# RWKV entry of a two-block forward pass: three receptance weight chunks multiplied as split fp32r products, and the elementwise chain behind them in another order

## What is computed

```python
xx = _token_shift(h) - h
xr, xw, xk, xv, xa, xg = [h + xx * mu[i] for i in range(6)]
r = (xr @ w_r).astype(f32)                      # the receptance
k = (xk @ w_k).astype(f32)
v = (xv @ w_v).astype(f32)
w = -jax.nn.softplus(-(w0 + jnp.tanh(xw @ w1) @ w2).astype(f32)) - 0.5
a = jax.nn.sigmoid((a0 + (xa @ a1) @ a2).astype(f32))
...
kk = kk / jnp.maximum(jnp.sqrt(jnp.sum(kk * kk, axis=-1, keepdims=True)), 1e-12)
k = k * (1.0 + (a - 1.0) * k_a.astype(f32))
decay = jnp.exp(-jnp.exp(w))
# step: sa = state @ a_t, with a_t = -kk; state = state * decay + sa b_t + v k; y = state @ r
bonus = jnp.sum(rh * kh * r_k.astype(f32), axis=-1, keepdims=True) * vh
```

## Time and profile before

| what | value |
|---|---|
| median of 3 runs | 1225.54 us (1224.85 to 1226.44) |
| the profiled execution | 1226.66 us, of which its span from first to last instruction is 1224.9 us |
| PE busy | 1211.5 us, 99% of the span |
| DVE, ACT, POOL busy | 523.5, 607.0 and 778.9 us |
| granted TensorE clock | 1.00 of full speed (2.4 GHz) over the span |
| the stretch that the change touches | about 853 to 915 us from the span's start |

### The profile page before, as it was taken

The page is one execution under the profiler, slowest core; times in us unless marked ns, Lnnn a source line. Parts: engine busy times, 40 slices in busy tenths (PEclk is TensorE's granted clock), DMA queues, the critical chain, the costliest instruction groups (busy, mean ns, idle before and its releaser), DMA issues.

```text
span 1224.9 us, 23270 instructions
## 1 busy us (share of the span) xinstructions
PE 1211.5 (99%) x9722; PEld 1055.7 (86%) x9722; DVE 523.5 (43%) x812; ACT 607.0 (50%) x793; POOL 778.9 (64%) x200
## 2 busy tenths in 40 slices
PE   8999999999999999999999999999999999999998
PEld 7888887788898888899988888888888998888887
DVE  4232234665433233243533332239696574332233
ACT  6544443545464445486465544455421445554543
POOL 3988880154188888766468888863015535888884
PEclk9999999999999999999999999999999999999999
DMA  7655554244255555555245555553332124555551
GB/s 295 210 199 187 189 195 159 73 174 170 71 191 208 184 202 178 202 189 182 74 143 196 184 195 190 187 186 124 138 138 71 38 92 154 181 197 200 180 203 68
DMA packets 31020, 202.01 MB, mean 165 GB/s; under 512 B 3424, under 2 KB 5344, under 8 KB 7392
## 3 DMA queue, kind: packets, MB, share of 16 engines
q1 hardware_dynamic: 28064, 196.63, 45.4%
q10 hardware_dynamic: 2880, 4.26, 1.0%
HBM read 198.79 MB, written 2.10 MB: 164 GB/s over the span
## 4 chain that ended last, share of the span: by engine, by line
PE 94%; POOL 2%; DVE 1%; issue 1%; ACT 1%; DMA 1%; SPq 0%; POOLq 0%; DVEq 0%
PE psum L353 25%; PE psum L355 13%; PE psum L344 10%; PE psum L346 10%; PE psum L345 10%; PE psum L986 6%; PE psum L999 3%; PE psum L3005 2%; POOL wlo L3384 2%; PE psum L3021 1%; PE psum L341 1%; PE psum L342 1%; PE psum L343 1%; PE psum L2975 1%; PE psum L599 1%
## 5 line engine op out<-in xcount | busy, mean ns | idle before, releaser
L3384 POOL TENSOR_TENSOR wlo<-raw,whi 128x2048 fp32r<-128x2048 f32 x160 | 736.6, 4609 | 282.2 <-ACT whi L314 237.6
L353 PE MATMUL psum<-f_both,whi 128*128 128x512 f32 x1408 | 492.2, 393 | 1.7 <-DVE wlo L699 1.7
L314 ACT ACTIVATE whi<-raw 128x2048 fp32r<-128x2048 f32 x160 | 306.3, 1915 | 218.5 <-PE psum L355 169.4
L355 PE MATMUL psum<-f_both,wlo 128*128 128x256 f32 x1408 | 393.7, 280 | 0.0
L353 PEld LDWEIGHTS psum<-f_both,whi 128*128 128x128 f32 x1408 | 264.4, 188 | 60.3 <-DVE wlo L699 2.2
L355 PEld LDWEIGHTS psum<-f_both,wlo 128*128 128x128 f32 x1408 | 264.5, 188 | 1.5
L344 PE MATMUL psum<-whi,ahi 128*128 128x512 f32 x352 | 137.4, 390 | 0.3 <-POOL wlo L3384 0.3
L346 PE MATMUL psum<-whi,alo 128*128 128x512 f32 x352 | 137.0, 389 | 0.0
L345 PE MATMUL psum<-wlo,ahi 128*128 128x512 f32 x352 | 136.9, 389 | 0.0
L909 DVE TENSOR_TENSOR psum<-psum,arena 128x512 f32<-128x512 f32 x43 | 30.1, 700 | 241.8 <-ACT arena L625 241.7
L925 DVE TENSOR_TENSOR alo<-arena,ahi 128x512 fp32r<-128x512 f32 x44 | 95.2, 2163 | 31.7 <-ACT ahi L858 31.7
(11 more groups left out here) (430 smaller groups left out, 1484.6 us busy)
## 6 DMA issues: line engine op xcount, KB each, us to landing
raw<-stream SPq DMA_DIRECT2D x182, 1024.0 KB, 4.8
con<-consts SPq DMA_DIRECT2D x1, 1376.0 KB, 14.6
x<-x_in SPq DMA_DIRECT2D x1, 1024.0 KB, 5.1
raw<-stream SPq DMA_DIRECT2D x2, 512.0 KB, 7.4
kept_x<-x ACTq DMA_DIRECT2D x1, 1024.0 KB, 3.9
x<-kept_x ACTq DMA_DIRECT2D x2, 512.0 KB, 3.9
out<-x SPq DMA_DIRECT2D x4, 256.0 KB, 2.0
arena<-gm_w_s ACTq DMA_DIRECT2D x1, 512.0 KB
```

Of the source, the lines that this page charges most:

```text
L314: nc.scalar.activation(whi[:, slot, :], raw[:, c % RAW, :], ACT.Copy).then_inc(high_made, 1)
L353: nc.tensor.matmul(psum[:, bank, :].rearrange("p (a n) -> p a n", a=2), whi[w], f_both[:, :, k, :], start=k == 0, stop=False, skip_group_c ...
L355: return nc.tensor.matmul(psum[:, bank, 0:TOK], wlo[w], f_hi[:, k, :], start=False, stop=k == KT - 1, skip_group_check=True)
L3384: nc.gpsimd.tensor_tensor(part(wlo[:, slot, :]), part(raw[:, c % RAW, :]), part(whi[:, slot, :]).bitcast(F32), ALU.subtract)\
```

## The change

It has four parts; two tensors `rx_hi` and `rx_lo` are laid into unused parts of the arena for it.

1. Receptance chunks 1, 2 and 3 are split chunks. ACT makes their high parts (in the loop of the sigmoids and behind the first two receptance copies) and four high parts `rx_hi` of their input; DVE, not POOL, makes their low parts (`receptance_low`) and the low parts `rx_lo` of the input. PE multiplies them with `split_by_tiles`.
2. The exponential of the sum before the token and the subtraction for it are dropped. The decayed keys take the exponential of the running sum, read one token earlier within each chunk of 64 tokens (L2620 of the changed kernel), and the first token of each chunk is only negated (L2619). Two exponentials are left.
3. The bonus weight r_k goes into the two-column matrix (`bonus_weights`), so that `rk` is a plain product in two instructions; the bonus sums stand behind value chunk 8 and the first half of value chunk 9. The bonus copy on DVE stands behind the low parts of chunk `L2`, and the first half of the first scores waits for `rw_scaled` 1 alone.
4. On ACT all four receptance copies stand ahead of the exponentials. The value mixture (variant 5) stands right behind the norms' reciprocal on DVE.

```diff
...
-RWKV_SPLIT = [("rw", 0, j) for j in (5, 6, 7)]
+RWKV_SPLIT = [("rw", 0, j) for j in (5, 6, 7, 1, 2, 3)]
...
+        bonus_weights = s3m[:, 384:400].rearrange("p (k h) -> p k h", k=8)
...
+            for b in range(4):
+                k = slice(2 * b, 2 * b + 2)
+                eng.wait_ge(s("rw_mixed"), mixed(4, 2 * b + 1))
+                nc.scalar.activation(rx_hi[:, k, :], variant_x[0][:, k, :], ACT.Copy).then_inc(s("rw_rhi"), 1)
             eng.wait_ge(s("rw_first"), 3)
...
             for k in range(8):
+                if k == 4:
+                    highs.upto(CH[RW(1)])
                 if k % 2 == 0:
...
                 projected(eng, name)
-                eng.wait_ge(s("rw_kx"), 4)
                 read(nc.scalar.activation(rr[:, 2 * j:2 * j + 2, :], bank2(proj_bank(name)), ACT.Copy), name)
-                if j == 0:
-                    eng.wait_ge(s("rw_before"), 1)
-                    nc.scalar.activation(sw, sw, ACT.Exp, scale=-DECAY).then_inc(s("rw_exp"), 1)
-                if j == 1:
-                    eng.wait_ge(s("rw_before"), 2)
+                if j < 2:
+                    highs.upto(CH[RW(2 + j)])
+                if j == 3:
+                    eng.wait_ge(s("rw_before"), 8)
                     nc.scalar.activation(sw, sums, ACT.Exp, scale=DECAY).then_inc(s("rw_exp"), 1)
-                    eng.wait_ge(s("rw_exp"), 2)
+                    eng.wait_ge(s("rw_exp"), 1)
                     nc.scalar.activation(sums, sums, ACT.Exp, scale=-DECAY).then_inc(s("rw_exp"), 1)
...
+            r_k = vec[:, VEC_AT["r_k"]:VEC_AT["r_k"] + 8].rearrange("p (k a) -> p k a", a=1).broadcast_to((P, 8, 2))
+            heads = const("same64")[:, 0:P:64].rearrange("p (a h) -> p a h", a=1).broadcast_to((P, 8, 2))
+            steps(nc.vector.tensor_tensor(bonus_weights, r_k, heads, ALU.mult))
             steps(nc.vector.memset(ht[:, :, 0:1], 0.0))
...
             nc.vector.reciprocal(roots[:, 0:2, :], roots[:, 0:2, :]).then_inc(s("rw_unit"), 1)
+            mix_variant(5)
+
+            def receptance_low(j):
 
-            eng.wait_ge(s("rw_sig"), 16)
+                c = CH[RW(j)]
+                eng.wait_ge(high_made, LOWS[c] - 2)
+                eng.wait_ge(low_made, LOWS[c] - 1)
+                nc.vector.tensor_tensor(wlo[:, SLOT[c], :], raw[:, c % RAW, :], whi[:, SLOT[c], :].bitcast(F32), ALU.subtract)\
+                    .then_inc(low_made, 1)
+
+            for b in range(4):
+                k = slice(2 * b, 2 * b + 2)
+                eng.wait_ge(s("rw_rhi"), b + 1)
+                nc.vector.tensor_tensor(rx_lo[:, k, :], variant_x[0][:, k, :], rx_hi[:, k, :].bitcast(F32), ALU.subtract)\
+                    .then_inc(s("rw_rlo"), 1)
+            receptance_low(1)
             for k in range(8):
-                ins = nc.vector.tensor_scalar(rr[:, k, :], aa[:, k, :], 1.0, V_AT("k_a", k), ALU.subtract, ALU.mult)
+                eng.wait_ge(s("rw_sig"), 2 * k + 2)
+                ins = nc.vector.tensor_scalar(sums[:, k, :], aa[:, k, :], 1.0, V_AT("k_a", k), ALU.subtract, ALU.mult)
             steps(ins)
...
    -                nc.vector.scalar_tensor_tensor(out=kx[:, k, :], in0=rr[:, k, :], scalar=1.0, in1=kx[:, k, :],
+                nc.vector.scalar_tensor_tensor(out=kx[:, k, :], in0=sums[:, k, :], scalar=1.0, in1=kx[:, k, :],
                                                op0=ALU.add, op1=ALU.mult).then_inc(s("rw_kx"), 1)
-            for k in range(8):
-                ins = nc.vector.tensor_tensor_scan(sums[:, k, :], const("restart", TOK), sw[:, k, :], 0.0, ALU.mult, ALU.add)
-            steps(ins)
-            nc.vector.tensor_tensor(sw, sums, sw, ALU.subtract).then_inc(s("rw_before"), 1)
+
+            def up_to_token(tiles):
+                for k in tiles:
+                    nc.vector.tensor_tensor_scan(sums[:, k, :], const("restart", TOK), sw[:, k, :], 0.0, ALU.mult, ALU.add)\
+                        .then_inc(s("rw_before"), 1)
+
+            eng.wait_ge(s("rw_kx"), 4)
+            up_to_token((0,))
+            receptance_low(2)
+            up_to_token((1, 2))
+            receptance_low(3)
+            up_to_token(range(3, 8))
             eng.wait_ge(S["rw_lw"], 6)
...
             steps(nc.vector.tensor_tensor(aa, aa, kk, ALU.mult))
-            eng.wait_ge(s("rw_exp"), 1)
-            nc.vector.scalar_tensor_tensor(out=kk, in0=kk, scalar=-1.0, in1=sw, op0=ALU.mult, op1=ALU.mult).then_inc(s("rw_before"), 1)
-            mix_variant(5)
+            chunks_of = lambda v: v.rearrange("p k (c t) -> p (k c) t", c=4)
             eng.wait_ge(s("rw_exp"), 2)
+            nc.vector.tensor_scalar(chunks_of(kk)[:, :, 0:1], chunks_of(kk)[:, :, 0:1], -1.0, None, ALU.mult)
+            steps(nc.vector.scalar_tensor_tensor(out=chunks_of(kk)[:, :, 1:64], in0=chunks_of(kk)[:, :, 1:64], scalar=-1.0,
+                                                 in1=chunks_of(sums)[:, :, 0:63], op0=ALU.mult, op1=ALU.mult))
             steps(nc.vector.tensor_tensor(aa, aa, sw, ALU.mult))
...
             eng.wait_ge(s("rw_mixed"), mixed(5, 7))
-            for k in range(8):
-                nc.vector.scalar_tensor_tensor(out=rk[:, k, :], in0=rr[:, k, :], scalar=V_AT("r_k", k), in1=kx[:, k, :],
-                                               op0=ALU.mult, op1=ALU.mult).then_inc(s("rw_rk"), 1)
+            for k in (slice(0, 4), slice(4, 8)):
+                nc.vector.tensor_tensor(rk[:, k, :], rr[:, k, :], kx[:, k, :], ALU.mult).then_inc(s("rw_rk"), 4)
             eng.wait_ge(s("rw_rk"), 8)
             steps(nc.vector.tensor_tensor(kx, kx, sw, ALU.mult))
-            eng.wait_ge(s("rw_exp"), 3)
             steps(nc.vector.tensor_tensor(rr, rr, sums, ALU.mult))
...
-            eng.wait_ge(s("rw_bonus_sum"), 1)
-            nc.vector.tensor_copy(bonus, psum[:, 4, 0:32]).then_inc(s("rw_scaled"), 1)
             eng.wait_ge(high_made, LOWS[L2] - 2)
...
                 .then_inc(low_made, 1)
+            eng.wait_ge(s("rw_bonus_sum"), 1)
+            nc.vector.tensor_copy(bonus, psum[:, 4, 0:32]).then_inc(s("rw_scaled"), 1)
             centred_values(0)
...
-            def split_by_tiles(slot, bank):
+            def split_by_tiles(slot, bank, h_hi=key_hi, h_lo=key_lo, made=lambda k: eng.wait_ge(s("rw_mixed"), 8 + k // 2 + 1)):
 
                 for k in range(KT):
-                    eng.wait_ge(s("rw_mixed"), 8 + k // 2 + 1)
+                    made(k)
                     for j in range(2):
                         w = (slice(None), slot, slice(k * 256 + j * P, k * 256 + j * P + P))
-                        mm = three_passes(bank2(bank)[:, j, :], whi[w], wlo[w], key_hi[:, k, :], key_lo[:, k, :], True,
+                        mm = three_passes(bank2(bank)[:, j, :], whi[w], wlo[w], h_hi[:, k, :], h_lo[:, k, :], True,
                                           (k, j) == (0, 0), k == KT - 1, skip=True)
...
             for j in range(1, 4):
-                project(eng, RW(j), plain_columns, h=variant_x[0])
+                project(eng, RW(j), split_by_tiles, h_hi=rx_hi, h_lo=rx_lo, made=lambda k: eng.wait_ge(s("rw_rlo"), k // 2 + 1))
                 if j == 1:
...
-            def bonus_sums(half, k):
+            def bonus_sums(k):
 
-                if half == 0:
-                    return
                 eng.wait_ge(s("rw_rk"), k + 1)
...
                     mm = nc.tensor.matmul(psum[:, 4, 16 * m + 2 * k:16 * m + 2 * k + 2], rk[:, k, m * P:(m + 1) * P],
-                                          const("same64")[:, 0:P:64], start=True, stop=True)
+                                          bonus_weights[:, k, :], start=True, stop=True)
                 if k == KT - 1:
...
-            project(eng, RW(8), plain_tokens, h=value_x, wait=made(5), between=bonus_sums)
+            project(eng, RW(8), plain_tokens, h=value_x, wait=made(5))
 
...
             values_quarter(1, 1)
+            for k in range(KT):
+                bonus_sums(k)
 
...
+            eng.wait_ge(s("rw_scaled"), 1)
+            scores(0, 0, 0)
             eng.wait_ge(s("rw_scaled"), 2)
-            for q in range(2):
-                scores(0, 0, q)
+            scores(0, 0, 1)
             values_quarter(1, 2)
...
                         rwkv_pool(pool, low)
-                    elif c not in PLAIN and names[c] not in (("lora", 0, 2), ("rw_o", 0, 1)):
+                    elif c not in PLAIN and names[c] not in (("lora", 0, 2), ("rw_o", 0, 1), RW(1), RW(2), RW(3)):
                         low(c)
```

6 lines of the change are left out of this document (4 added, 2 removed).

## The result

The changed kernel takes 1228.62 us in the median of 10 runs (1227.41 to 1230.11), the kernel before beside it on the same chip 1225.5 us (10 runs, 1224.51 to 1226.51). The ratio is 1.0026, with a 95% interval of 1.0016 to 1.0035: the change makes the kernel 3.1 us slower. The forecast of 1227.1 us had the sign and half of the size. The profiled execution took 1230.11 us, 3.45 more than the one of before; its span is 1228.2 us against 1224.9. It is the longest of the ten, so the traces show how the time is made up, and the medians what the change costs.

The account below looks back on a forecast made before the run. The prediction took PE, with 94% of the chain, to bound the kernel. PE -3.6, bank's wait -0.6, late low part +0.2 and PE idle +5.6 gave +1.6 on 1225.54, so 1227.1 us; range 1224.6 to 1229.8.

Parts of the forecast that it names:

- The low part of receptance 1: Ahead of the first split receptance chunk: DVE has it at 873.3, PE comes at 875.7, in time by 2.4 us.
- the 3.6 us of three chunks: Receptance chunks 1 to 3 on PE: split chunks take 5.85 us instead of 7.04, giving back 3.6 us.
- its chain: DVE's operations behind the exponentials, from negated first tokens to the small copy: 12.0 us, to 912.5; between 11.5 and 13.2.
- The sum of the forecast: Over the entry: PE -3.6, bank's wait -0.6, late low part +0.2, PE idle around the scores +5.6, giving +1.6 us.
- its own three pieces: PE's idle pieces before and between the two halves of the scores: about 1.2, 2.5 and 1.6 us.
- the forecast's own band: Whole kernel: a change between +0.8 and +2.4 us, with chance 0.54.
- the first two rivals: Before the scores, the clock falls: 1229.5 us, chance 0.14; or the entry is later than summed: 1228.9 us, chance 0.13.
- one of the forecast's signs of being wrong: In the profile after 905: a granted clock under 1.00 would show the forecast wrong; no size given.
- cost the same wherever they stand: Bonus sums on PE: their 32 two-column records take 3.55 us in any place.
- The first rival: Before the scores: PE's pauses lower the clock to half, 2.4 us more on top of +1.6, 1229.5 us; chance 0.14.
- what follows keeps its order and is bound by PE, so the delay stays: Behind the scores and the start of the solve: nothing is added, the delay of +1.6 us stays.
- PE's saving arrives in full: Rival for the entry: the chain behind the last receptance product is hidden, -4.2 us, 1221.3 us; chance 0.06.

Follow-up runs that it names:

- e3: The changed kernel with receptance chunks 1 to 3 plain again, without high and low parts: 1233.33 us, ratio 1.0054 to the kernel before.
- e1: The changed kernel with both exponentials on ACT ahead of the last receptance copy: 1226.01 us, ratio 0.9996 to the kernel before.
- e7: The kernel before with only the bonus sums moved, in one block behind the first half of value chunk 9: 1230.41 us, ratio 1.0028.
- e9: The changed kernel with 16 small constant products (64 instructions) added in PE's idle time at the kernel's start: 1229.74 us, ratio 1.0032 to the kernel before.
- e12: The kernel before with 24 small constant products (96 instructions) added in PE's idle time at the start: 1226.69 us against 1226.56, ratio 1.0002.
- e6: The changed kernel with exponentials ahead of the last receptance copy and bonus sums laid between the value products: 1225.0 us, ratio 0.9983 to the kernel before.
- e10: e6 with 16 small constant products (64 instructions) added at the kernel's start: 1223.59 us, ratio 0.9974 to the kernel before.
- e11: e6 with 24 small constant products (96 instructions) added at the kernel's start: 1222.36 us, ratio 0.9971 to the kernel before.
- e8: The changed kernel with the bonus sums laid between the value products, exponentials still behind the last copy: 1236.8 us, ratio 1.008 to the kernel before.

## Why the prediction was right, and where it was wrong

**Right: the path.** The low part of receptance 1 was there 2.3 us before PE came to it (2.4 forecast), and only receptance 2 had to wait for its own, by some 0.1 us (0.2 forecast). A split receptance chunk took 5.9 us (875.08 to 880.99; 5.85 forecast), and e3 confirms the 3.6 us of three chunks with 3.4. The last copy came at 893.91 (894.7 forecast), table load and exponentials ended at 899.7 (900.5), DVE idled 5.61 us (5), its chain took 12.0 us (12.0) and the small copy came at 911.6 (912.5). All of it ran 0.8 us early, 0.45 of which it had from the start of the stage. That DVE's chain is the bound is shown by e1, where it is moved and the waits go.

**Mis-sized: the idle time and what the clock adds.** The sum of the forecast had -4.0 us for PE ahead of the idle pieces, +5.6 of PE idle (its own three pieces, 1.2, 2.5 and 1.6, add up to 5.3) and nothing for the clock. Measured from the sums of squares on, value chunk 8 starts 4.3 us sooner, PE is idle for 1.60 + 1.85 + 0.60 = 4.05 us, and the bonus sums and scores keep it busy for 0.6 and 1.7 us longer: -4.3 + 4.05 + 2.3 = +2.1. The last two terms belong together: most of what the clock added filled idle time that was there anyway, and only some 0.8 us of it was new. In the end the measured +3.1 us lie outside the forecast's own band of +0.8 to +2.4 and inside the stated range, which had room for the first two rivals: that the time lies in the range is owed to this room and not to the sum. And one of the forecast's signs of being wrong came true, a granted clock under 1.00 after 905.

The forecast had each half of the scores at 1.0 us. They took 1.99 and 1.73. The sentence that the bonus sums "cost the same wherever they stand" is wrong: 3.55 us among the value products, 4.17 in a row here and 4.69 in e7. In the changed kernel much of this is hidden, since PE waits for DVE anyway: the first half of the scores was done before the bonus copy, so only the second half's 1.73 - 1.0 = 0.7 us stands in the path (914.19 for the copy, 913.84 for the end of the first half). That, with what was early, makes +2.1 in the entry where +1.6 was forecast. The first rival had the effect, a falling clock, and priced it at 2.4 us on top of the whole idle time, too much for this place. Its price stood on no low clock at all: the ten records of 4.63 us in the earlier trace rows ran with a granted clock of 1.00, and the same ten took 3.94 us in the changed kernel, at 1.00 as well. As the cause it named the pauses, which is at most half of it. I had argued against it with a single pause of 1.67 us that did no harm, and never asked what products of two columns do to the clock. No row of the kernel before could show it, since it has them spread.

**Wrong: "what follows keeps its order and is bound by PE, so the delay stays".** It shrank by 0.4 us before 963 and grew by 2.0 behind it. Of the 2.0, 1.1 are stops (1.8 against 0.8 of the kernel before) whose places have moved, since the change adds products ahead of them; e9 shows that they are places. For the rest, about 0.9, I have no row of its own, but it comes with the places too, since e12 has a like rest without any change. What decides how long a stop is stays open: the profiled executions of all kernels here have between 0.8 and 2.4 us of them, the kernel before the least. So the stops are in the profiled difference of 3.3 us of span; how much of the 3.1 us between the medians is theirs isn't shown, e9, with the stops elsewhere, came out no faster, and e12, with more of them, no slower in the median.

**The rivals.** "PE's saving arrives in full", -4.2 us, would have needed DVE four us sooner, and the order stood in the way. With the exponentials ahead of the last copy and the bonus sums spread, the entry of e6, e10 and e11 does come out at -3.8. The saving was there; two placements gave it away.

## What to carry to other kernels

The same work doesn't cost PE the same in every place: before moving a group of very narrow matmuls into one row, ask what surrounds them, and keep them between wide ones. When a product is made faster, look at what is queued behind it on the engines that read it; here the two exponentials needed nothing of the last receptance copy, and stood behind it. And when the bound moves from PE to a chain of other engines, a long pause of PE can cost twice, once as waiting and again in the clock behind it, as in e8; in short pauses a low clock can also cost little, as in e9, since PE has to wait in any case.

## What the runs showed of the hardware

- The granted clock falls to 0.50 without any idle time of PE, inside or right behind 16 two-column matmuls (32 records) in a row: e7 (PE 6.00 of 6.00 us busy ahead of it) and e1 (4.00 of 4.00). It was back at 1.00 by 912 in e1 and by 918 in e7, in both behind the scores and the first value products. The same 32 records four at a time between value products leave it at 1.00 (e6, e10, e11).
- 5.15 us of idle time do it too (e8), and there the clock stayed at 0.50 until 921.7, though PE was busy nearly all the while (7.39 of 7.50 us from 905 on).
- At the kernel's start the clock fell at 11.3 us behind pauses of 0.95 and 2.16 us in the changed kernel, and stayed at 1.00 behind 0.38 and 1.67 us in the kernel before.
- PE stops for 0.1 to 1.2 us at places of its program whole multiples of 256 instructions apart, where its products are of 64 x 64 (50 stops in fourteen traces); 64 instructions added 850 us earlier move them (e9).
- An operation of DVE with all operands in SBUF ran slower beside POOL: L2688, 128 x 512, took 1.62 us from 917.01 on, beside POOL's L3308 (914.30 to 918.08), and 0.68 us in the kernel before (L2655), as POOL's work ended. L2686 and L2687 beside it, which read PSUM, kept 0.68 and 0.69.
